# Gate products of a recurrence: from two full-array products per block to four 64 by 64 quarters of the TensorE array

## The reference

```
proj = x @ w_in + b_in                      # 1024 -> 7 * 1024
xa, ga, b_gate, c_gate, v_sc, m_a, m_b = split(proj)
xc  = causal_dwconv(xa, ..., conv_a_w) + conv_a_b
xb  = xc.reshape(b, s, 16, 64)              # 16 heads of 64 channels
r   = sigmoid(einsum("bshi,hij->bshj", xb, lru_wa) + lru_ba)
i   = sigmoid(einsum("bshi,hij->bshj", xb, lru_wx) + lru_bx)
log_a = -8 * r * softplus(-lam);  a = exp(log_a)
b   = sqrt(-expm1(2 * log_a)) * (i * xc)
h   = scan: h = a * h + b                   # over the positions
y_a = h * gelu(ga)
y_b = b_gate * causal_dwconv(c_gate * v_sc, ...)
mixed = (sigmoid(m_a) * y_a + sigmoid(m_b) * y_b) @ w_out
x = layernorm(ALPHA * x + mixed)
x = layernorm(ALPHA * x + moe_ffn(x))       # top 4 of 32 experts, w_gu 1024 x 2048, w_down 1024 x 1024
```

## Time and profile before

| | us |
|---|---|
| median of 3 runs | 1187.73 (1187.62 to 1188.11) |
| profiled execution, its own time | 1189.59 |
| its span, first to last instruction | 1187.8 |
| PE busy | 1143.1 (96%) |
| DVE busy | 523.5 (44%) |
| ACT busy | 264.7 (22%) |
| POOL busy | 3.3 |

### The profile page before, as it was taken

The page is one execution under the profiler, slowest core; times in us unless marked ns, Lnnn a source line. Parts: engine busy times, 40 slices in busy tenths (PEclk is TensorE's granted clock), DMA queues, the critical chain, the costliest instruction groups (busy, mean ns, idle before and its releaser), DMA issues.

```text
span 1187.8 us, 14041 instructions
## 1 busy us (share of the span) xinstructions
PE 1143.1 (96%) x5715; PEld 563.7 (47%) x5715; DVE 523.5 (44%) x997; ACT 264.7 (22%) x410; POOL 3.3 (0%) x13
## 2 busy tenths in 40 slices
PE   9999999999999999999999989999999999999994
PEld 8999999773333333333333333333333333333331
DVE  6798899982333333333333333333333333333336
ACT  5655666421111111111111111111111111111112
POOL 1000000000000000000000000000000000000000
PEclk9999999999999999999999999999999999999997
DMA  9867644899999999999999999999999999999993
GB/s 231 224 212 210 180 143 130 308 411 381 422 428 428 426 429 427 427 429 426 429 425 429 426 428 428 426 428 428 427 427 427 427 428 427 429 426 429 426 424 130
DMA packets 93854, 443.80 MB, mean 374 GB/s; under 512 B 7912, under 2 KB 65400, under 8 KB 68062
## 3 DMA queue, kind: packets, MB, share of 16 engines
q1 hardware_dynamic: 93614, 442.41, 92.2%
q10 hardware_dynamic: 176, 0.48, 0.1%
HBM read 441.34 MB, written 1.53 MB: 373 GB/s over the span
## 4 chain that ended last, share of the span: by engine, by line
PE 74%; DMA 23%; DVE 1%; ACT 1%; issue 0%; DVEq 0%; SPq 0%
PE PS L951 25%; DMA ring<-in_w_gu 19%; PE PS L748 17%; PE PS L986 13%; PE PS L868 6%; DMA ring<-in_w_down 4%; PE PS L890 3%; PE PS L783 2%; PE PS L876 1%; PE PS L883 1%; PE PS L923 1%; PE PS L1026 1%; PE PS L758 1%; PE PS L957 1%; PE PS L767 1%; PE PS L927 1%
## 5 line engine op out<-in xcount | busy, mean ns | idle before, releaser
L951 PE MATMUL PS<-ring,mid 128*64 128x512 f32 x1920 | 422.1, 593 | 18.3 <-DMA ring<-in_w_gu 17.7
L951 PEld LDWEIGHTS PS<-ring,mid 128*64 128x64 f32 x1920 | 135.8, 137 | 297.7 <-issue 260.5
L986 PE MATMUL PS<-ring,mid 128*64 128x512 f32 x952 | 210.8, 595 | 0.0
L1443 DVE TENSOR_SCALAR PS<-PS 128x512 f32<-128x512 f32 x30 | 21.0, 700 | 351.6 <-PE PS L951 351.6
L748 PE MATMUL PS<-x_hi,w_hi 128*128 128x320 f32 x448 | 140.7, 314 | 0.4 <-DVE w_lo L1093 0.4
L748 PE MATMUL PS<-x_lo,w_hi 128*128 128x320 f32 x448 | 139.0, 310 | 0.0
L748 PE MATMUL PS<-x_hi,w_lo 128*128 128x320 f32 x448 | 138.9, 310 | 0.0
L1429 DVE TENSOR_TENSOR ys<-PS,ys 64x512 fp32r<-64x512 f32 x64 | 44.1, 689 | 201.6 <-ACT ys L653 193.2
L986 PEld LDWEIGHTS PS<-ring,mid 128*64 128x64 f32 x952 | 65.8, 137 | 129.9 <-issue 129.9
L1136 DVE SCALAR_TENSOR_TENSOR x_tok<-PS,gate,x_tok 128x1024 f32<-128x1024 f32 (+1 forms) x93 | 114.9, 1275 | 21.3 <-PE PS L890 21.3
L644 ACT ACTIVATE mid<-PS 128x512 f32<-128x512 f32 x30 | 17.9, 597 | 416.8 <-DVE PS L1443 416.8
(11 more groups left out here) (246 smaller groups left out, 785.0 us busy)
## 6 DMA issues: line engine op xcount, KB each, us to landing
ring<-in_w_gu SPq DMA_DIRECT2D x124, 2048.0 KB, 42.1
ring<-in_w_down SPq DMA_DIRECT2D x59, 2048.0 KB, 40.7
raw<-in_w_in SPq DMA_DIRECT2D x56, 512.0 KB, 5.2
ring<-in_w_down SPq DMA_DIRECT2D x9, 1024.0 KB, 15.2
ring<-in_w_gu SPq DMA_DIRECT2D x8, 1024.0 KB, 7.3
ring<-in_w_out SPq DMA_DIRECT2D x4, 1024.0 KB, 5.5
x_tok<-in_x_prompt SPq DMA_DIRECT2D x2, 512.0 KB, 5.3
x_tok<-in_w_down SPq DMA_DIRECT2D x1, 1024.0 KB, 15.7
```

The costliest lines, as they stand in the source:

```text
L951: last = mm(PS[64 * a:64 * a + 64, b, :], xgT[:, 2 * (u % 2) + j, u // 2, :], w[2 * j + b][:, a * HALF:(a + 1) * HALF], start=False, stop= ...
L986: last = mm(PS[64 * a:64 * a + 64, XB, :], hT[:, j, u, :], w[j][:, a * HALF:(a + 1) * HALF], start=False, stop=(u == 1 and j == 3))
L1443: dve.tensor_scalar(gm, gm, LIMIT, None, ALU.min).then_inc(gm_ok, 1)
```

## The change

The two gate products of a block become four, each of one head's 64 by 64 weights: head 0 reads array rows 0 to 63, head 1 rows 64 to 127; the output goes to columns 0 to 63 or 64 to 127, `a ^ head`, so that the four take the four different quarters of the array. Head 0 writes PSUM bank 6, head 1 bank 7. One `gates_done` follows the last of them. `wab` holds only the heads' weights (half the size), so the memset of zeros and SP's wait for it go, and DVE's copy to `wcur` is of 128 instead of 256 columns. ACT takes the gates in four pieces of 64 partitions, the two of the r gate first, then one of the i gate, the tanh of r, and the last of the i gate. DVE does `aa = tr + 1` first and then waits for the i gate.

```diff
-        wab = x1[:, 0:2, :].rearrange("p a (c n) -> p a c n", c=KC)
+        wab = x1[:, 0, :].rearrange("p (a c n) -> p a c n", a=2, c=KC)
...
-            sp.wait_ge(zero_ok, 1)
...
-                    sp.dma_start(wab[64 * j:64 * j + 64, a, :, 64 * j:64 * j + 64],
+                    sp.dma_start(wab[64 * j:64 * j + 64, a, :, :],
...
-            pool.memset(wab, 0.0).then_inc(zero_ok, 1)
...
-                    act.wait_ge(gates_done, 2 * c + 2)
-                    act.activation(ti, PS[:, 7, 0:T], ACT.Tanh, bias=ghalf[:, KC + c:KC + c + 1], scale=0.5)\
-                       .then_inc(gates_taken, 1)
-                    act.activation(tr, PS[:, 6, 0:T], ACT.Tanh, bias=ghalf[:, c:c + 1], scale=0.5)\
-                       .then_inc(gates_taken, 1)
-                    act.wait_ge(gates_taken, 2 * c + 4)
+                    def gate_rows(dst, a, head):
+
+                        rows, at_rows = slice(64 * head, 64 * head + 64), slice(64 * (a ^ head), 64 * (a ^ head) + 64)
+                        return act.activation(dst[rows, :], PS[at_rows, 6 + head, 0:T], ACT.Tanh,
+                                              bias=ghalf[rows, a * KC + c:a * KC + c + 1], scale=0.5)
+
+                    act.wait_ge(gates_done, c + 1)
+                    gate_rows(tr, 0, 0)
+                    gate_rows(tr, 0, 1).then_inc(gates_taken, 1)
+                    gate_rows(ti, 1, 0)
+                    act.wait_ge(gates_taken, 2 * c + 3)
                     act.activation(tr, tr, ACT.Tanh, bias=sp2[:, c:c + 1], scale=sp2[:, c:c + 1]).then_inc(t_ok, 1)
+                    gate_rows(ti, 1, 1).then_inc(gates_taken, 1)
...
                     for a in range(2):
-                        mm(PS[:, 6 + a, 0:T], wcur[:, a, :], xc, start=True, stop=True).then_inc(gates_done, 1)
+                        for head in range(2):
+                            rows, out = slice(64 * head, 64 * head + 64), slice(64 * (a ^ head), 64 * (a ^ head) + 64)
+                            last = mm(PS[out, 6 + head, 0:T], wcur[rows, a, :], xc[rows, :], start=True, stop=True)
+                    last.then_inc(gates_done, 1)
...
-                stt(ti, ti, 1.0, xc, ALU.add, ALU.mult)
-                link(dve.tensor_scalar(aa, tr, 1.0, None, ALU.add))
+                dve.tensor_scalar(aa, tr, 1.0, None, ALU.add)
+                dve.wait_ge(gates_taken, 2 * c + 4)
+                link(stt(ti, ti, 1.0, xc, ALU.add, ALU.mult))
```

More of the change, by code:

```diff
@@ L183, in hybrid_layer @@
         PS = ctx.enter_context(nc.psum_tensor("PS", [P, 8, HALF], F32))
-        tiles = place("tiles", [P, 12 * T + 2 * P], 5 * slot)
+        tiles = place("tiles", [P, 12 * T + P], 5 * slot)
         bgt, cgt, vt, gel, tma, tmb, xc, tr, ti, rr, aa, sq = (tiles[:, i * T:(i + 1) * T] for i in range(12))
-        wcur = tiles[:, 12 * T:12 * T + 2 * P].rearrange("p (a n) -> p a n", a=2)
+        wcur = tiles[:, 12 * T:12 * T + P].rearrange("p (a n) -> p a n", a=2)
         hh = rr
@@ L1162, in constants @@
                                       ALU.add, ALU.add)
-                dve.wait_ge(zero_ok, 2)
+                dve.wait_ge(zero_ok, 1)
                 dve.tensor_copy(items[0:1, 0, 0:3], iota[0:1, PREV - 1:PREV + 2])
```

## The result

| | before | after |
|---|---|---|
| median of all runs, us | 1187.85 (22 runs, 1185.78 to 1189.90) | 1190.87 (22 runs, 1189.43 to 1192.20) |
| ratio, 95% interval | | 1.0026 [1.0020, 1.0032] |
| profiled execution: time / span, us | 1189.6 / 1187.8 | 1190.2 / 1188.4 |
| from one block's gates to the next's, us | 25.71 | 26.18 |
| first gates to first output projection, us | 181.14 | 184.07 |

The change makes the kernel 3.0 us slower. The forecast was 1186.0 with a range up to 1188.8: the time lies outside, on the other side. The two profiled executions differ by 0.6 us only. The stretch from the first gates to the first output projection grew by 184.07 - 181.14 = 2.93 us, as the medians did.

A forecast was written before the change was run, and what follows sets the result against it. PE bounds the kernel until about 294 us, then the weight stream; PE's gains before 220 us reach the end. Gate products save 0.19 us seven times plus 0.40, sum 1.7, other terms nothing: 1187.7 to 1186.0, range 1184.0 to 1188.8.

The forecast's parts named there:

- What bounds the kernel: Whole kernel: PE until about 294 us, then the weight stream; PE gains before 220 us come out at the end.
- The gate products: PE, each block: two waves plus division changes, 0.89 us against 1.08; 0.19 saved seven times, 0.40 at the last.
- Rivals 1 (four waves): PE gate products: row halves don't overlap, 1.43 us a block, +2.6 us, 1190.3; chance 0.10.
- 2 (five): PE gate products: records keep strictly to program order, 1.69 us a block, +4.7 us, 1192.4; chance 0.05.
- rival 3: PE gate products: change of division costs little, up to 4.3 us saved, 1183.4; chance 0.08.
- ACT: Gate reads: 0.84 us more a block, start 0.40 earlier, next high part 0.2 to 0.3 later; cost 0.
- The failed step: ACT's late high part: its piece is multiplied 10.6 us later, so nothing on the path waits; cost 0.
- the sentence on DVE: DVE, each block: a round 0.19 us shorter plus 0.3 for the late high part, 0.5 of 1.9 us idle.
- Rival 4: Projection blocks: ACT's longer round or DVE's last block takes PE's place; no change, 1187.7; chance 0.11.
- The start: Kernel start: POOL's 1.80 us memset goes but ends before PE's first transpose; gains nothing.
- DVE behind the last block: After the eighth block: `mix_lo` keeps 0.5 us of its 0.9 before PE wants it; PE still later.

The follow-up runs named there:

- e4: Changed kernel with ACT and DVE as before (two reads of 128 partitions, i gate first; gates computed wrong): 1185.90 us, ratio 0.9983.
- e5: Changed kernel with ACT's next high part made right behind the last gate read, ahead of table load and square root: 1187.33 us, ratio 0.9991.
- e6: Changed kernel with ACT's high part ahead of the root and DVE's sixth low part ahead of the convolution: 1186.27 us, ratio 0.9989.
- e3: Kernel before, full-array gate products, with only the change's ACT and DVE side (four reads of 64 partitions): 1193.98 us, ratio 1.0051.
- e7: Changed kernel with ACT's second and third gate reads exchanged: 1191.82 us (one run).
- e1: Changed kernel with DVE making the sixth piece's low part before the convolution of xc instead of behind it: 1187.11 us, ratio 0.9992.
- e2: Kernel before with DVE making the sixth piece's low part before the convolution of xc: 1187.43 us, ratio 0.9995.
- e8: Kernel before with ACT's next high part moved ahead of the table load and square root: 1187.95 us, ratio 0.9997.

## Why the prediction was wrong

**What bounds the kernel: right, but read without its lead.** PE alone stood on the chain of before, and a gain or a loss before 220 us does come out at the end. Over the eight timed kernels the change of the stretch (+2.93, -0.95, -0.02, +6.26, -1.36, -1.36, -1.36, -0.02) and that of the median (+3.0, -0.7, -0.4, +6.2, -1.9, -0.5, -1.6, +0.1) go together within 0.9 us, the intervals being 0.7 to 1.6 us to either side. The chain names who is last; it does not say by how little the next is earlier.

**The gate products: the mechanism right, the saving 0.06 a block too high.** In the trace after, the four first records of a block start at 142.569, .575, .582 and .589, the four second ones at 142.889 to 142.909: two waves 0.32 us apart (the rows below give all eight as one).

```profile
142.33 0.31 PE L752 MATMUL PS<-x_hi,w_lo 128*128 128x320 f32 x1
142.57 0.77 PE L764 MATMUL PS<-tiles 64*64 64x320 f32 x8
143.35 0.38 PE L752 MATMUL PS<-x_hi,w_hi 128*128 128x320 f32 x1
143.57 0.31 PE L752 MATMUL PS<-x_lo,w_hi 128*128 128x320 f32 x1
```

From the last full product's start to the second one's after it is 1.24 us (143.57 - 142.33); before it was 1.37 (143.04 - 141.67). So 0.13 is saved and not 0.19. At the last block it is 0.38, as put (0.40). 7 x 0.13 + 0.38 = 1.29; e4 and e5 measured 1.36, because their stretch begins with the first gate record and so leaves out the 0.09 that the way in costs at the first block. Rivals 1 (four waves) and 2 (five) are refuted by the starts, rival 3 (no cost of division, 0.54 saved a block) by the 0.13. The Trainium skill ("TensorE: Matmul & The Clock Gate", Part 3, The mechanism) has matmuls start in program order; here all four products' first records start before any second one, so the trace does not agree if a product's two records stand together in the program.

**ACT: a term mis-sized.** "The square root and the next high part (146.43) come about 0.2 to 0.3 later": it was 0.71. The forecast's own prices give more than it wrote: 0.84 for two more reads less 0.40 for the earlier start is 0.44. The rest are the prices. The first three reads put the tanh 1.51 us behind the first (0.98 before), and the fourth, which starts when the tanh has ended, adds another 0.53; the distance of 0.42 had been taken from reads of 128 partitions, where the earlier trace rows gave only how long one read of 64 takes. Together 4.39 us from first read to high part against 3.33 before, which is 1.06 and not 0.84, less 0.35 and not 0.40 for the earlier start.

**The failed step.** "Nothing on the path waits for that: the piece that this feeds is multiplied three products (10.6 us) later. Cost 0". That piece does have its 10 us. But the late high part holds up DVE, which makes its low part next and then everything else in order: the recurrence, the next block's convolution, and the low part of the sixth piece, which had a lead of 0.28 us. I followed the data of the late instruction and not the engine queue behind the one that waits for it. With it fell the sentence on DVE, "together 0.5 of 1.9 us of idle". The idle time of 1.22 us stands *ahead* of the low part and is the wait for the high part itself; it moves with the high part and absorbs nothing. The slack that counts lies behind it, where DVE hands over to PE, and that was 0.28. Even the forecast's own 0.3 us on ACT would have made the round 25.43 + 0.3 = 25.73, a little over before's 25.71, and eaten the gain of the seven blocks.

**The price.** 26.18 - 25.71 = 0.47 a block, 7 blocks 3.3 us, less 0.38 for the last: 2.9, as measured. Rival 4 ("the saving stays in a wait", 1187.7) names ACT's longer round and is the right kind, but the margin that it gives for itself is that of the last block, and its price ends at the loss of the gain. A round that becomes longer than PE's period is a loss without that ceiling; no rival had it.

**The start: right. DVE behind the last block: a term mis-sized.** The missing memset shows nowhere. DVE's `mix_lo` was to keep 0.5 us of its 0.9 before PE wants it; in after it ends at 234.60 and PE goes on at 234.69, so 0.1 is left. PE does not wait there, but some 2.2 us further on it loses 0.19 us waiting for the low part of `w_out` that DVE makes next:

```profile
PEld PS L790 <- DVE out_lo L1308: 0.3, 1, 0.3
```

All kernels with four reads have this wait, also e5 and e6, and none with two reads. It lies behind the stretch and is not in its 2.93 us. The stream still turns saturated at 290 to 300 us (428 GB/s from 300 us on):

```profile
290.00:300.00 10.00, 10.00 (x50) 3.43 (x48) 3.98 (x9) 1.18 (x2) 0.00 (x0) 1.00 0.97 392
```

## What to carry to other kernels

When an engine off the path comes later, follow the queue behind whatever waits for it, once round through all engines and back to the engine on the path, and compare the sum with the period: the difference, here 0.28 of 25.7 us, is the only slack, and idle time inside the round is none. List for every piece that is handed over in the loop when it is ready and when it is wanted; the smallest lead sets what an edit may cost. When such a lead is used up, look for work in the round that nobody in it waits for (here a table load and a square root) and put it behind.

## What the hardware showed that was not expected

**Reads of 64 partitions.** They cost ACT more than those of 128 when they follow each other: 0.53 to 0.55 us from start to start against 0.42 for 320 columns (after, e3, e5 and e7 against before and e4), although one takes the same 0.52 to 0.53. Halving these two tiles by partitions so costs 1.06 us a block, not 0.84. The number of partitions alone does not decide it. In after the tanh of 128 partitions, which writes from partition 0 as the third read does, starts 0.10 us before that read has ended (144.92 against 145.02); in e5 the high part of 128 partitions, behind a read that writes from partition 64, starts only after it (144.73 against 144.70). Where of two activations around the gates the second waits for nothing and still does not overlap the first, they differ in the partition at which they write or at which they read PSUM. Two reads of 64 partitions that agree in both were not tried, so this rule fits but is not shown.

**PE's clock at the start.** In the profiles of before, e1, e3, e4, e5 and e6 the stretch of 10 to 20 us shows a granted clock of 0.83; in those of after, e2, e7 and e8 it shows 1.00. In before the granted clock is 1.00 up to 11.6 us, 0.50 (the lower level, 1.2 GHz) until 15.0, and 1.00 again. Some 9 to 14 records more than in the others start 0.27 us apart instead of 0.15; that is 1.1 to 1.6 us. Before and after:

```profile
11.60:15.00 3.40, 3.15 (x12) 3.15 (x13) 3.32 (x7) 1.67 (x4) 0.00 (x0) 0.50 0.92 249
```

```profile
11.60:15.00 3.40, 3.04 (x21) 3.04 (x22) 3.40 (x7) 1.72 (x5) 0.00 (x0) 1.00 0.98 258
```

Kernels with and without the quarters and with and without each edit stand on both sides, so it follows neither; there is one profile of each kernel, so that it belongs to the execution is likely and not shown. It is half of why two single profiles of kernels 3 us apart differ by 0.6, and why a stretch that begins after it, or the median, has to be compared. What decides it is open. Open too is the other half, the end: from the start of the output projection to the end of the span the profiled executions take 965.6 to 967.9 us, by no order that these runs explain. The clock does not sort them: before (967.7) and e2 (965.6) both show 1.00 from 20 to 1170 us.
